# Attention probabilities transposed by a product with a scaled identity

## The reference

```python
s = einsum('bgrtd,bgnd->bgrtn', q, k_cmp) * scale          # branch 0: 31 compressed keys
p_cmp = softmax(where(cvalid, s, NEG)) * any_valid
o_cmp = einsum('bgrtn,bgnd->bgrtd', p_cmp, v_cmp)
# branch 1: the 16 best blocks of 64 keys, causal
p = softmax(where(kpos <= tpos, (q @ k_s) * scale, NEG)); o_slc = p @ v_s
# branch 2: a window of 512 keys, causal
pw = softmax(where(mw, (q @ k_w) * scale, NEG));           o_win = pw @ v_w
gates = sigmoid(g_pre)                                      # one per token, head, branch
o = gates[..., 0:1] * o_cmp + gates[..., 1:2] * o_slc + gates[..., 2:3] * o_win
```

## Time and profile before

| | us |
|---|---|
| median of 3 runs | 2765.18 |
| lowest, highest | 2763.38, 2765.46 |
| profiled execution, whole | 2762.43 |
| its span | 2760.6 |
| TensorE busy | 2646.3 (96%) |
| VectorE busy | 1672.2 (61%) |
| ScalarE busy | 687.5 (25%) |

### The profile page before, as it was taken

The page is one execution under the profiler, slowest core; times in us unless marked ns, Lnnn a source line. Parts: engine busy times, 40 slices in busy tenths (PEclk is TensorE's granted clock), DMA queues, the critical chain, the costliest instruction groups (busy, mean ns, idle before and its releaser), DMA issues.

```text
span 2760.6 us, 30304 instructions
## 1 busy us (share of the span) xinstructions
PE 2646.3 (96%) x11868; PEld 1981.8 (72%) x11868; DVE 1672.2 (61%) x2950; ACT 687.5 (25%) x1301; POOL 166.7 (6%) x126
## 2 busy tenths in 40 slices
PE   4999999999999999999999999998999899999999
PEld 1566666668888887888887888884455455788888
DVE  1566666478776555455647777646375376666552
ACT  1333334131111022112103111005352254322200
POOL 0010001010000020000001000002132000000000
PEclk8999999999999999999999999999999999999999
DMA  8122112125443321221122454331111220222121
GB/s 332 42 92 92 62 62 92 61 87 196 161 168 145 115 103 65 81 77 65 62 92 95 180 183 164 125 123 38 44 61 61 92 92 1 92 92 80 56 103 52
DMA packets 24492, 275.00 MB, mean 100 GB/s; under 512 B 3480, under 2 KB 4376, under 8 KB 7072
## 3 DMA queue, kind: packets, MB, share of 16 engines
q1 hardware_dynamic: 19440, 266.45, 25.8%
q10 hardware_dynamic: 4912, 6.63, 0.7%
HBM read 270.97 MB, written 2.10 MB: 99 GB/s over the span
## 4 chain that ended last, share of the span: by engine, by line
PE 90%; DVE 5%; DMA 2%; ACT 1%; issue 1%; POOL 0%; ACTq 0%; DVEq 0%; POOLq 0%
PE bank L526 29%; PE bank L608 14%; PE bank L2127 10%; PE bank L1247 8%; PE bank L2528 4%; PE bank L401 4%; PE bank L1914 4%; PE bank L1377 2%; PE bank L1395 2%; PE bank L2212 1%; PE bank L2911 1%; PE bank L2521 1%; PE bank L2648 1%; DMA ones<-in_ones 1%; PE bank L2993 1%
## 5 line engine op out<-in xcount | busy, mean ns | idle before, releaser
L526 PE MATMUL bank<-HT,ring 128*128 128x256 f32 x1056 | 253.5, 387 | 9.8 <-ACT HT L935 7.4
L1247 PE MATMUL bank<-HT,ring 128*128 128x512 f32 x512 | 250.3, 597 | 5.6 <-ACT arena L1529 5.6
L526 PE MATMUL bank<-arena,ring 128*128 128x256 f32 x1056 | 249.5, 379 | 0.0
L526 PE MATMUL bank<-arena 128*128 128x256 f32 x1056 | 249.5, 379 | 0.0
L526 PEld LDWEIGHTS bank<-HT,ring 128*128 128x128 f32 x1056 | 203.1, 194 | 45.7 <-issue 15.5
L526 PEld LDWEIGHTS bank<-arena,ring 128*128 128x128 f32 x1056 | 200.6, 190 | 27.3
L526 PEld LDWEIGHTS bank<-arena 128*128 128x128 f32 x1056 | 200.6, 190 | 27.3
L608 PE MATMUL bank<-arena,ring 128*128 128x256 f32 x936 | 207.3, 380 | 9.3 <-ACT arena L680 5.6
L608 PEld LDWEIGHTS bank<-arena,ring 128*128 128x128 f32 x936 | 177.0, 190 | 37.0 <-ACT arena L680 6.8
L1175 ACT ACTIVATE arena<-bank,ffc 128x512 f32<-128x512 f32 x66 | 51.3, 778 | 485.2 <-DVE bank L1083 485.2
L2528 PE MATMUL bank<-HT,ring 128*128 128x512 f32 x320 | 147.7, 598 | 3.0 <-ACT HT L975 3.0
(11 more groups left out here) (465 smaller groups left out, 4321.2 us busy)
## 6 DMA issues: line engine op xcount, KB each, us to landing
ring<-w_ada SPq DMA_DIRECT2D x33, 2048.0 KB, 8.1
ring<-w_up SPq DMA_DIRECT2D x33, 2048.0 KB, 7.8
ring<-w_down SPq DMA_DIRECT2D x24, 1408.0 KB, 5.9
ring<-w_gdn SPq DMA_DIRECT2D x8, 2048.0 KB, 8.6
ring<-w_ret_qk SPq DMA_DIRECT2D x4, 2048.0 KB, 8.0
ring<-w_ret_v SPq DMA_DIRECT2D x4, 2048.0 KB, 7.6
ring<-w_ret_g SPq DMA_DIRECT2D x4, 2048.0 KB, 7.7
ring<-w_ret_out SPq DMA_DIRECT2D x4, 2048.0 KB, 7.6
```

What stands on the lines that cost most here:

```text
L526: last = nc.tensor.matmul(out_, w[:, k, :], x[:, k, :], start=(first and k == 0), stop=(k == 3), skip_group_check=not first)
L1247: last = nc.tensor.matmul(B[u % 2][:, :], w[:, u, k, :], HT[:, k, :], start=(k == 0), stop=(k == KC - 1))
```

## The change

For branches 1 and 2 the probabilities stay unscaled. VectorE multiplies the 128x128 identity by reciprocal and gate instead, into one of two new tiles per group (`scaled_ident[n % 2][:, g, :]`), whatever the width of the item. TensorE replaces the transposition by an ordinary product of the unscaled probabilities (stationary) with this scaled identity (moving): out[k, q] = sum over p of P[p, k] x S[p, q] = P[q, k] x scale[q]. VectorE waits, before it overwrites a scaled identity, for the products that read it two items before. Branch 0 keeps both its scaling and its transpositions.

```diff
+        scaled_ident = [region(o + m * 2 * P, 2, P) for m in range(2)]; o += 4 * P
...
                     for j in range(NT if b == 0 else i + 1):
-                        last = nc.tensor.transpose(B4[2 + g][:, j, :], Pn[n % 3][:, 4 * g + j, :], ident[:, :])
+                        if b == 0:
+                            last = nc.tensor.transpose(B4[2 + g][:, j, :], Pn[n % 3][:, 4 * g + j, :], ident[:, :])
+                        else:
+                            last = nc.tensor.matmul(B4[2 + g][:, j, :], Pn[n % 3][:, 4 * g + j, :], scaled_ident[n % 2][:, g, :], start=True, stop=True)
                     last.then_inc(pe_done, PE.tick("nsa", "pt", n, g))
...
                     for g in range(NG):
                         head = NG * 2 * g + r
-                        p = Pn[n % 3][:, 4 * g:4 * g + i + 1, :].rearrange("p j c -> p (j c)")
-                        nc.vector.tensor_scalar(p, p, small[:, c + g:c + g + 1], VSW[:, i, 256 + 3 * head + b:257 + 3 * head + b],
+                        if n >= 2:
+                            dve.wait_ge(pe_done, at("pe", "nsa", "pt", n - 2, g))
+                        nc.vector.tensor_scalar(scaled_ident[n % 2][:, g, :], ident[:, :], small[:, c + g:c + g + 1], VSW[:, i, 256 + 3 * head + b:257 + 3 * head + b],
                                                 ALU.mult, ALU.mult).then_inc(dve_done, DV.tick("nsa", "p", n, g))
```

## The result

The changed kernel takes 2776.05 us (median of 6 runs, 2773.03 to 2778.69), the kernel before 2765.32 (6 runs, 2762.35 to 2773.57). The ratio is 1.0035 with a 95% interval of 1.0019 to 1.0050: slower by 10.7 us, with 5 to 14 us inside the interval. The profiled execution took 2776.26 us, against 2762.43.

The account below looks back on a forecast made before the run. TensorE was taken as the main bound, idle about 1.6 us per round; 4 x 3.01 + 0.23 - 0.03 = 12.2 us on 2762.4 gave 2774.6, plus 2.8 to the median 2777 us, range 2771 to 2783.5.

Parts of the forecast that it names:

- 2 of (1,0), before L2975: Branch 1, tile 0: two products add 0.225 us into TensorE's 0.37 us idle before L2975, so 0 per round.
- 4 of (1,1) and the start of (1,2): Four products add 0.45 us into 0.67 idle; VectorE, 0.134 shorter, still sets the start: -0.13 us per round.
- 6 of (1,2): Branch 1, tile 2: six products add 0.675 us, less 0.07 for the second group's scaling: +0.61 us per round.
- 8 of (1,3): Branch 1, tile 3: TensorE is late, so eight products count in full, +0.90 us per round.
- 2 of (2,0): Branch 2, tile 0: two products add +0.225 us per round.
- 4 of (2,1), 6 of (2,2): Ten products add 1.125 us, less idle 0.52 and 0.09 that they fill: +0.51 us per round.
- 8 of (2,3): Branch 2, tile 3: eight products add +0.90 us per round.
- The wait that was added: VectorE waits for item n-2 before overwriting a scaled identity; tightest at (2,0), some 1.5 us left, costed at nothing.
- the full price: Rival: TensorE pays all 160 products at 0.1125 us, no idle time filled: 18.0 us, 2783 us; 11%.
- The win of VectorE's relief: Rival: relief before (1,2) and (2,3) saves 2.4 us in all, 2762.8 us, if products cost what transpositions do; 3%.
- The product of four passes: Rival: each product takes 0.435 us in place of 0.108, 46 us in all, 2811 us; 3%.
- More is hidden: Rival: more of the added work is hidden than counted, under 5.5 us slower in all; 7%.

Follow-up runs that it names:

- relief_only: Also experiment 1: the changed kernel, but TensorE still transposes with the plain identity, VectorE scaling the identity; loop 86.80 us, 2760.70 us, ratio 0.9991.
- experiment 7: The changed kernel with VectorE's reciprocal and scaling for items (1,2) and (2,2) ahead of the next item's mask and maximum; loop 101.14 us, 0.95 less than the change.
- experiment 4: The kernel before with ordinary plain-identity products only for items (1,0) and (1,1), 24 of 160, probabilities scaled in place; loop 89.55 us, +0.30.
- experiment 5: The kernel before with ordinary plain-identity products only for item (1,3), 32 of 160, probabilities scaled in place; loop 93.08 us, +3.83.
- experiment 8: The changed kernel with unscaled probabilities and scaled identity of branches 1 and 2 rounded to bfloat16, one instruction per product; 2755.41 us, ratio 0.9972.

## Why the prediction was right

The forecast was 2777 us, measured were 2776.05. That the two are so close is in part luck: for its own execution the sum gives 2774.6, and 2776.26 were measured, since the loop came out 0.6 us longer than 12.2 and 1.1 us more lie outside it, where nothing was changed; the 2.8 us added to get from the execution to the median made up for it, and they came from few runs of the kernel before. What held is the way there, term by term. The distances in the table are from start to start on TensorE, by the timelines of before and after. Beside the earlier trace rows, these rows of the round before give their ends:

```profile
2255.99 0.66 PE L2993 MATMUL bank<-ident,arena 128*128 128x128 f32 x4
...
2258.98 0.66 PE L2979 MATMUL bank<-arena 128*64 128x128 f32 x8
...
2261.22 0.88 PE L2979 MATMUL bank<-arena 128*64 128x128 f32 x12
...
2263.24 1.09 PE L2979 MATMUL bank<-arena 128*64 128x128 f32 x16
...
2265.33 0.66 PE L2993 MATMUL bank<-ident,arena 128*128 128x128 f32 x4
...
2270.95 0.88 PE L2979 MATMUL bank<-arena 128*64 128x128 f32 x12
```


| step, per round | predicted | measured |
|---|---|---|
| 2 of (1,0), before L2975 | 0 | 0.00 (0.81 in both) |
| 4 of (1,1) and the start of (1,2) | -0.13 | -0.13 (2.12 to 1.99) |
| 6 of (1,2) | +0.61 | +0.66 (0.87 to 1.53) |
| 8 of (1,3) | +0.90 | +0.96 (1.02 to 1.98) |
| 2 of (2,0) | +0.225 | +0.27 (0.37 to 0.64) |
| 4 of (2,1), 6 of (2,2) | +0.51 | +0.43 (4.58 to 5.01) |
| 8 of (2,3) | +0.90 | +0.94 (1.04 to 1.98) |
| a round | 3.01 | 3.14 |
| the loop | 12.2 | 12.84 |

The loop is four rounds of 3.14 and 0.29 for the first round's (1,0), for which I had 0.23. The price per product was mis-sized by a little: the steps give 0.96 / 8 = 0.120 us where TensorE is late, not 0.1125. The 0.1125 is half of a pair; "an added pair less one transposition", as I called it, is 0.225 - 0.1075 = 0.1175. I had also counted nothing per group; the groups of two, four, six and eight take 0.64, 1.09, 1.53 and 1.98 us, which is 0.223 per product and 0.19 per group, and transpositions 0.37, 0.59, 0.87 and 1.02, which is 0.108 each and 0.15 per group (the six have 0.07 more, the second group's scaling, which is gone in relief_only's 0.80). So a product costs 0.115 more than a transposition and a group of them 0.04 more; what the 0.04 are no run shows. The one term that came out lower, 0.43 for 0.51, is the idle time in front of (2,2) and (2,3): I subtracted what the brackets gave, and the products filled more: the starts after L2959 and L2963 came 0.16 and 0.59 us nearer, 0.75 in place of the brackets' 0.61. A bracket begins at the end of a row, which lies some 0.07 us behind the point from which the next could have started (a row of 0.66 us is followed 0.59 us later); it is what I missed in experiment 7 too.

That added work is worth only what stands where the engine is late was the core of the forecast, and experiments 4 and 5 show it with one and the same operation: 0.30 us for all 24 in the idle places, and those in the first round alone, 0.120 each in the late ones. The wait that was added cost nothing, as forecast (experiment 1 contains it). The overlap of two neighbouring VectorE instructions, which I had put at 0.07 us, is 0.09 (2 x 0.343 - 0.60), and the waits didn't end it. Of the signs, TensorE's busy time in the loop rose by 18.6 us (80.90 to 99.54), just over the 15 to 18 named.

The rivals: the full price (18 us) was wrong since experiment 4's places are free. The win of VectorE's relief exists in kind, 2.45 us in experiment 1, but needs a product for less than 0.028 us more than a transposition, and the fp32 product is 0.120 more. In experiment 8, where the product is cheaper than the transposition, the change as a whole is a gain. The product of four passes was not so: eight take 1.98 us, against 1.02 for eight transpositions, a factor of two. The factor of four that the Trainium skill's "TensorE: Matmul & The Clock Gate", section Terms, states for FP32 is not what these runs show between a transposition and an ordinary product. My argument against it, that every fp32 product of this trace is two instructions at 0.11 us, is right in the two, but the 0.11 holds for this shape alone: L2979's, with 64 columns in the stationary tile, are 0.055 us each. "More is hidden" was not so.

The median moved by 10.7 us and the loop of the profiled executions by 12.84; the ratio's interval (5 to 14 us) holds both, and the 12.2 to 13.4 us against the later runs of the kernel before speak for the second.

## What to carry to other kernels

In float32 a transposition is one instruction and an ordinary product two: folding a scale into the transposition by an ordinary product doubles TensorE's part, and saves VectorE a part of one pass. Count first on which engine the stage waits, place by place: a saving on the other engine is worth the idle time that it ends (here 2.45 of 6.4 us, and 0.6 once that idle time was filled). Where bfloat16 is precise enough, the same fold is a gain over the fp32 kernel, since the product is then cheaper than the fp32 transposition; whether it beats bfloat16 transpositions without a fold is not shown.

## What the runs showed of the hardware

- An ordinary product of 128x128 by 128x128 costs 0.223 us in a stream in fp32 (two instructions, weight loads of 191 ns: four products take 1.09 and eight 1.98 us), a transposition 0.108 (one, 140 to 144 ns: 0.59 and 1.02 us), a bfloat16 product 0.055 (one, 97 ns: 0.33 and 0.55 us). I had reckoned with a transposition's price for the last, or little less.
- The price of an fp32 instruction follows the stationary tile too: with the same 128 moving columns it is 0.112 us at 128 stationary columns (L2997) and 0.055 at 64 (L2979: eight take 0.59 and sixteen 1.03 us).
- A VectorE multiplication of 128x128 took 344 ns from SBUF to SBUF whether it wrote float32 or bfloat16.
- Two VectorE instructions of 128 columns in a row take 0.60 us whether the second waits for a semaphore (L3149) or not (L3144), so that the added wait, which was always met by then, didn't end their overlap.
